# A two-layer hybrid trunk on one core: token differences in other buffers, and two weight splits of each head pair on GpSimd

## What is computed

```
h = rms_norm(x, g);  z = h @ w_in[l]                       # 2048 -> 6400 columns
z_rwkv = z[:, :3328] + (previous token's z - z) * mu       # "token shift"
y_r = rwkv7(r, k, v, decay, a, gate)                       # 16 heads x 64, chunked delta rule
y_a = causal attention with rotary q, k                    # 8 heads x 128, 256 keys
x = x + rms_norm([y_r, y_a] @ w_out[l], g)
x = x + rms_norm(relu(h2 @ w_up[l])**2 @ w_down[l], g)     # 2048 -> 8192 -> 2048
```

## Time and profile before

| | |
|---|---|
| median of 3 runs | 2717.87 us (2716.47 to 2718.49) |
| the profiled execution | 2718.53 us, span 2716.9 us |
| busy share of the span | PE 96%, PEld 79%, DVE 62%, ACT 45%, POOL 4% |
| mean granted TensorE clock | 0.985 |
| DMA | 419.96 MB, 155 GB/s over the span |

### The profile page before, as it was taken

One profiled execution on the slowest core, in us unless ns is written; L12 is line 12 of the kernel. 1 busy time (PEld: TensorE's weight loads), 2 busy tenths in 40 slices (PEclk: granted clock), 3 DMA queues, 4 the chain that ended last, 5 costly groups with the idle time before them and its releaser, 6 DMA issues.

```text
span 2716.9 us, 48417 instructions
## 1 busy us (share of the span) xinstructions
PE 2612.0 (96%) x16267; PEld 2137.8 (79%) x16267; DVE 1680.0 (62%) x2761; ACT 1213.9 (45%) x1896; POOL 116.8 (4%) x183
## 2 busy tenths in 40 slices
PE   7999999999999999999899999999999999999998
PEld 6777777777888888888787777776778888888886
DVE  5666666656656556566566666666576565565665
ACT  5444444445434444444454444444454344344443
POOL 3000000000000000000010000000000000000000
PEclk9999999999999999999999999999999999999999
DMA  6333333355555555555533333333555555555554
GB/s 196 100 110 103 102 102 103 103 179 170 190 195 179 197 191 185 193 186 186 181 112 105 108 97 101 103 103 101 179 164 197 192 186 189 192 185 193 178 196 151
DMA packets 437897, 419.96 MB, mean 155 GB/s; under 512 B 19502, under 2 KB 351936, under 8 KB 437824
## 3 DMA queue, kind: packets, MB, share of 16 engines
q1 hardware_dynamic: 434176, 412.49, 47.8%
q0 software_dynamic: 3648, 6.52, 0.8%
HBM read 416.84 MB, written 2.10 MB: 154 GB/s over the span
## 4 chain that ended last, share of the span: by engine, by line
PE 87%; DVE 7%; issue 2%; ACT 2%; POOL 1%; DVEq 0%; DMA 0%; SPq 0%; ACTq 0%; POOLq 0%
PE gemm_bank L515 27%; PE gemm_bank L516 14%; PE gemm_bank L540 11%; PE gemm_bank L542 11%; PE gemm_bank L541 11%; PE gemm_bank L518 2%; DVE b_wlo L1157 1%; PE mix_banks L662 1%; PE mix_banks L688 1%; ACT b_whi L893 1%; DVE b_rn L1268 1%; PE mix_banks L695 1%; PE mix_banks L734 1%; PE mix_banks L738 1%; PE mix_banks L745 1%
## 5 line engine op out<-in xcount | busy, mean ns | idle before, releaser
L1157 DVE TENSOR_TENSOR b_wlo<-b_raw,b_whi 128x1024 fp32r<-128x1024 f32 x777 | 940.1, 1223 | 593.5 <-ACT b_whi L893 591.3
L515 PE MATMUL gemm_bank<-b_hT,b_whi 128*128 128x512 f32 x3420 | 1268.5, 411 | 5.2 <-DVE b_zt L1163 5.0
L893 ACT ACTIVATE b_whi<-b_raw 128x1024 fp32r<-128x1024 f32 x777 | 810.0, 1057 | 609.9 <-PE gemm_bank L542 423.6
L516 PE MATMUL gemm_bank<-b_hT,b_wlo 128*128 128x256 f32 x3648 | 1018.4, 283 | 0.0
L515 PEld LDWEIGHTS gemm_bank<-b_hT,b_whi 128*128 128x128 f32 x3420 | 649.4, 190 | 177.4 <-issue 24.6
L516 PEld LDWEIGHTS gemm_bank<-b_hT,b_wlo 128*128 128x128 f32 x3648 | 695.8, 191 | 11.5
L540 PE MATMUL gemm_bank<-b_whi,b_mT 128*128 128x512 f32 x1280 | 501.6, 392 | 0.0
L542 PE MATMUL gemm_bank<-b_whi,b_mT 128*128 128x512 f32 x1280 | 498.3, 389 | 0.0
L541 PE MATMUL gemm_bank<-b_wlo,b_mT 128*128 128x512 f32 x1280 | 498.2, 389 | 0.0
L540 PEld LDWEIGHTS gemm_bank<-b_whi,b_mT 128*128 128x128 f32 x1280 | 240.3, 188 | 51.3 <-issue 1.4
L542 PEld LDWEIGHTS gemm_bank<-b_whi,b_mT 128*128 128x128 f32 x1280 | 240.3, 188 | 50.1
(11 more groups left out here) (236 smaller groups left out, 1915.5 us busy)
## 6 DMA issues: line engine op xcount, KB each, us to landing
b_raw<-in_w_up SPq DMA_DIRECT2D x256, 512.0 KB
b_raw<-in_w_down SPq DMA_DIRECT2D x256, 512.0 KB
b_raw<-in_w_in SPq DMA_DIRECT2D x384, 256.0 KB
b_raw<-in_w_out SPq DMA_DIRECT2D x60, 512.0 KB
b_raw<-in_w_in SPq DMA_DIRECT2D x8, 512.0 KB
b_xt<-in_x SPq DMA_DIRECT2D x4, 512.0 KB, 6.0
b_raw<-in_w_out SPq DMA_DIRECT2D x8, 256.0 KB
out<-b_xt SPq DMA_DIRECT2D x8, 256.0 KB, 2.3
```

The lines of the kernel that those rows point to most:

```text
L515: mm(bank[b0 + b][:, :], whi[r][:, cols], pair, start=first, stop=False)
L516: m = mm(bank[b0 + b][:, 0:SEQ], wlo[r][:, cols], act[:, kt, 0, :], start=False, stop=False)
L893: f(whi[r][:, :], raw[r][:, :, :].rearrange("p a b -> p (a b)"), ACT.Copy).then_inc(hi_done, 1)
L1157: tt(wlo[r][:, :], flat(raw[r][:, :, :]), whi[r][:, :].bitcast(F32), ALU.subtract).then_inc(lo_done, 1)
```

## The change

`dsh` becomes three separate buffers: `ta` and `kf` for the two differences of line 441, and the second half of `xs` for the third. The first two are last read at lines 1298 to 1310 of the same pair. `pt` moves to the first 384 columns of `yo`. GpSimd no longer waits for TensorE's transpose (`x_free`) ahead of line 441; the semaphore keeps only its use at the start, under the name `col_zero`. TensorE's `key_norms` moves from behind lines 776 and 777 to ahead of the wait for the probabilities. DVE's `step(-1)` and `step(10)` are gone; GpSimd makes these two `lo` splits of each pair, between the first two differences and the third, each after the matching `hi` and in the order of `lo_done`. DVE waits for both at `step(0)`.

```
-        pt = yof[:, 768:1152]
+        pt = yof[:, 0:384]
-        dsh = yof[:, 0:3 * SEQ].rearrange("p (a b) -> p a b", b=SEQ)
+        dsh = (ta[:, :], kf[:, :], xs[:, 1, :])
...
-            def unit(l, i, n, tiles, after):
+            def unit(l, i, n, tiles, slot, after):
                 pool.wait_ge(tile_out, tiles - 2)
-                pool.wait_ge(e["x_free"], n + 1)
                 for j in (1, 0):
-                    nc.gpsimd.tensor_tensor(dsh[:, j, :], zt[:, j, 0:SEQ], zt[:, j, 1:SEQ + 1],
+                    nc.gpsimd.tensor_tensor(dsh[j], zt[:, j, 0:SEQ], zt[:, j, 1:SEQ + 1],
                                             ALU.subtract).then_inc(e["diffed"], 1)
+                for j in range(2):
+                    pool.wait_ge(hi_done, slot + j + 1)
+                    pool.wait_ge(lo_done, slot + j)
+                    at = (start[l, "pairs"][0] + 9 + j) % ROUND
+                    nc.gpsimd.tensor_tensor(wlo[at][:, :], raw[at][:, :, :].rearrange("p a b -> p (a b)"),
+                                            whi[at][:, :].bitcast(F32), ALU.subtract).then_inc(lo_done, 1)
                 pool.wait_ge(e["pair_done"], n + 1)
                 pool.wait_ge(tile_out, tiles)
...                                        (TensorE, tail of a pair)
                 for u in range(2):
                     m = turned(mb[1][:, P * u:P * u + P], zt[:, 5, 1 + P * u:1 + P * u + P], ident)
-                    m.then_inc(e["va_turned"] if u else e["x_free"], 1)
+                m.then_inc(e["va_turned"], 1)
+                if more:
+                    key_norms(n + 1)
                 pe.wait_ge(e["probs"], V)
...
                 mm(mb[1][:, P:2 * P], vt[:, 1, :], pt[:, 2 * P:3 * P], ...).then_inc(e["o_sum"], 1)
-                if more:
-                    key_norms(n + 1)
                 fill(2)
...                                        (DVE)
                 nc.vector.tensor_tensor_scan(flat(cs[:, :, :]), hp, flat(ldc[:, :, :]), 0.0, ...)
-                step(-1)
...
                 step(9)
-                step(10)
...
                     def step(j):
+                        if j == 0:
+                            dve.wait_ge(lo_done, k + 8 + LEAD + i * 12)
                         lo(k + 8 + j + LEAD, i * 3)
```

More of the change, by code:

```diff
@@ L227, in trunk @@
                  "u_sum", "u_out", "s_sum", "s_tmp", "s_out", "y_sum", "y_mean", "y_cen", "y_sq", "y_var", "y_root",
-                 "y_rinv", "y_norm", "y_turned", "y_gain", "y_bonus", "y_scaled", "y_gated", "y_hi", "x_free",
+                 "y_rinv", "y_norm", "y_turned", "y_gain", "y_bonus", "y_scaled", "y_gated", "y_hi", "col_zero",
                  "swapped", "roped_c", "roped_s", "roped", "va_turned", "va_out", "score_sum", "masked", "smax",
@@ L409, in _ @@
             nc.gpsimd.memset(yof, 0.0).then_inc(clears, 1)
-            nc.gpsimd.memset(ldc[:, :, 0:1], 0.0).then_inc(e["x_free"], 1)
+            nc.gpsimd.memset(ldc[:, :, 0:1], 0.0).then_inc(e["col_zero"], 1)
             nc.gpsimd.memset(St[:, 0, :], 0.0).then_inc(e["pair_done"], 1)
@@ L434, in _ @@
             pair_weights(0, 0)
-            def unit(l, i, n, tiles, after):
+            def unit(l, i, n, tiles, slot, after):
                 pool.wait_ge(tile_out, tiles - 2)
-                pool.wait_ge(e["x_free"], n + 1)
                 for j in (1, 0):
-                    nc.gpsimd.tensor_tensor(dsh[:, j, :], zt[:, j, 0:SEQ], zt[:, j, 1:SEQ + 1],
+                    nc.gpsimd.tensor_tensor(dsh[j], zt[:, j, 0:SEQ], zt[:, j, 1:SEQ + 1],
                                             ALU.subtract).then_inc(e["diffed"], 1)
+                for j in range(2):
[4 more added lines that the diff above has]
+                                            whi[at][:, :].bitcast(F32), ALU.subtract).then_inc(lo_done, 1)
                 pool.wait_ge(e["pair_done"], n + 1)
                 pool.wait_ge(tile_out, tiles)
-                nc.gpsimd.tensor_tensor(dsh[:, 2, :], zt[:, 2, 0:SEQ], zt[:, 2, 1:SEQ + 1],
+                nc.gpsimd.tensor_tensor(dsh[2], zt[:, 2, 0:SEQ], zt[:, 2, 1:SEQ + 1],
                                         ALU.subtract).then_inc(e["diffed"], 1)
@@ L484, in _ @@
                 k, t = start[l, "pairs"]
-                loop(pool, PAIRS - 1, lambda i: unit(l, i, PAIRS * l + i, t + 4 + i * 6,
+                loop(pool, PAIRS - 1, lambda i: unit(l, i, PAIRS * l + i, t + 4 + i * 6, k + 9 + i * 12,
                                                      lambda: pair_weights(l, i + 1)))
-                unit(l, PAIRS - 1, PAIRS * l + PAIRS - 1, t + 6 * PAIRS - 2,
+                unit(l, PAIRS - 1, PAIRS * l + PAIRS - 1, t + 6 * PAIRS - 2, k + 93,
                      lambda: pair_weights(l + 1, 0) if l < DEPTH - 1 else None)
@@ L1250, in key_norms @@
                     dve.wait_ge(e["diffed"], 3 * n + m + 1)
-                    stt(sh[:, j, :], dsh[:, j, :], col(MU + PAIRS * j), zt[:, j, 1:], ALU.mult,
+                    stt(sh[:, j, :], dsh[j], col(MU + PAIRS * j), zt[:, j, 1:], ALU.mult,
                         ALU.add).then_inc(e["shifted"], 1)
@@ L1286, in mixer @@
                 dve.wait_ge(e["diffed"], 3 * n + 3)
-                stt(sh[:, 2, :], dsh[:, 2, :], col(MU + PAIRS * 2), zt[:, 2, 1:], ALU.mult,
+                stt(sh[:, 2, :], dsh[2], col(MU + PAIRS * 2), zt[:, 2, 1:], ALU.mult,
                     ALU.add).then_inc(e["shifted"], 1)
@@ L1473, in parameters @@
                 dve.wait_ge(clears, 2)
-                dve.wait_ge(e["x_free"], 1)
+                dve.wait_ge(e["col_zero"], 1)
             for l in range(DEPTH):
@@ L1504, in _ @@
                 sums(t, 0, place(0))
-                for j in range(3):
+                for j in range(2):
                     lo(k + 4 + LEAD + j)
@@ L1523, in step @@
                 def step(j):
+                    if j == 0:
+                        dve.wait_ge(lo_done, k + 92 + LEAD)
                     if j < 10:
```

## The result

The changed kernel takes 2649.33 us (median of 4 runs, 2648.75 to 2650.53); the kernel before took 2717.49 us beside it (4 runs, 2716.47 to 2718.49). The ratio is 0.975, interval 0.9733 to 0.9767. The profiled execution took 2648.75 us against 2718.53: 69.8 us less, where 69 were forecast; between the medians it is 68.2 us.

A forecast was written before the change was run, and what follows sets the result against it. TensorE, busy 96% of the span, was taken as the bound, leaving only its idle time and half-clock stretches. 41.5 + 22 + 8.5 - 3 = 69 us off 2718.53 gave 2649.5, stated as 2650; range 2637 to 2664.

The forecast's parts named there:

- The stall: TensorE's wait at the transposes of the probabilities, 14 times 3.0 us, goes entirely: 41.5 us.
- Rival C: The stall only moves: key norms' products or line 786 hold TensorE for 2 of 3 us; 2688, chance 0.08.
- What is late next: Tail, line 786, normalised output: a looped pair has about 0.5 us of cover, so no wait, narrowly.
- The clock: Half-clock windows of TensorE behind the stalls vanish with them: 22 us, bounds 0 and 22.
- Rival B: The stall goes but TensorE's clock still falls at the same places for another reason: 2671, chance 0.08.
- Size of GpSimd's split: A 128 x 1024 `lo` split on GpSimd takes 2.45 us, four times the 613 ns row, and stays hidden.
- rival A: Slow splits at the pair's start: 3.9 us each on GpSimd, TensorE waits at line 650; 2686, chance 0.13 with E.
- D: Slower than before: GpSimd's splits above 5.2 us become the chain through the third difference; 2765 at 6 us, chance 0.05.
- E: GpSimd is held by another wait (`lo_done` or `pair_done`) and behaves as rival A; chance 0.13 together with it.
- DVE relieved: Without `step(10)` and `step(-1)`, TensorE's waits shrink: 2.5 us at line 515, 5 at 650, 1 at 640; 8.5 together.
- New contention: In the tail, GpSimd's first differences delay DVE's chunk-state updates by 0.2 us each: 3 us lost, bounds 0 and 8.
- The key norms' move: TensorE's two key-norm products go ahead of the probabilities; costed at nothing in the sum.

The follow-up runs named there:

- busy_stall: Kernel before, plus four throwaway TensorE products of 384 columns in the stall ahead of the probabilities' transposes; 2695.81 us, ratio 0.9919.
- moved_no_gpsimd: Changed kernel with the two splits of a pair back on DVE, key norms' move and new buffers kept; 2647.09 us, ratio 0.9737.
- splits_only: Kernel before with only the two splits of a pair on GpSimd; buffers, transpose wait and key norms' order as before; 2723.19 us, ratio 1.0022.
- floor_early_both: Changed kernel, both splits on GpSimd, with DVE's floor under the key norms moved ahead of `step(9)`; 2652.22 us, ratio 0.9765.
- floor_early_none: Changed kernel with all splits back on DVE and DVE's floor under the key norms moved ahead of `step(9)`; 2641.66 us, ratio 0.9722.

## Why the prediction was right, and where it was wrong

The sum was 41.5 + 22 + 8.5 - 3 = 69, and 69.8 came (68.2 by the medians). By the medians of the runs it is 42.1 (stall) + 22.6 (clock) + 6.7 (key norms moved) - 3.7 (GpSimd's splits), 67.7. It was right in its total because the two large terms were right; that is the mechanism. That the rest came out within 2.5 us (8.5 - 3 = 5.5 forecast, 6.7 - 3.7 = 3.0 measured) is luck: neither of the two terms was what it was taken for.

*The stall.* Right, with both margins near the forecast: GpSimd was 1.1 us ahead of DVE (104.93 and 106.03; 1.1 forecast), and DVE waited 0.98 us for ACT (0.7 forecast). Two signs were misstated, and decide nothing. Line 1251 was to start "some 3.9 us after `zt`"; by the prediction's own times that is 2.3 us after (3.9 or so is how much earlier it comes), and 2.36 was measured. And 64.4 us is the first looped pair's length; the mean was 63.66. Rival C (the stall only moves) is excluded by the missing waits at lines 621 and 778.

*What is late next.* Right: no looped pair waits at line 791, as forecast for line 786.

*The clock.* Right, and shown by busy_stall: 22.6 us against 22. Rival B (no clock) falls.

*Size of GpSimd's split.* Right: 2.38 us against 2.45 from the row of 613 ns. Rivals A and D needed 3.9 us and over 5.2. The third difference was hidden, as the forecast had it: DVE's line 1291 has no wait for it. With that E falls too.

*DVE relieved, 8.5 us.* Wrong. The step that failed is "Removing `step(-1)` brings line 1310 forward by up to 1.2 us". It brought it forward by 1.2 and put it back by 1.4. At line 650, where 5 us were to be won, nothing was (7.1 and 7.1; all eight of these waits are in layer 1); at line 640, where 1 us was, 2.7 were lost. Only the 2.5 us at line 515 came, and even these are not due to `step(10)` alone: moved_no_gpsimd, in which DVE has all its splits, has the same 2.2 us there, from the moved key norms; in splits_only it was the missing `step(10)`.

*New contention, 3 us.* Wrong in its place. It was looked for in the tail, where the chunk-state update at line 1402 takes 0.35 us as it did before: it starts only as GpSimd's second difference ends, and the update ahead of it (line 1399) has an input in PSUM. It lay at the start of the pair, beside the long splits. The prediction had the two rows (613 and 977 ns) and read them as GpSimd's price only; it never asked what the same meeting costs DVE, and called DVE's work there "mostly one-input" and so exempt. The trace of the kernel before already held the answer, in layer 1, where GpSimd's value residual runs beside DVE:

```profile
1417.91 0.48 DVE L1295 SCALAR_TENSOR_TENSOR b_rn<-b_sh,b_drv,b_rn 128x256 f32<-128x256 f32 x1
...
1417.97 1.00 POOL L451 TENSOR_TENSOR b_xs<-b_vf,b_sh 128x256 f32<-128x256 f32 x1 [5.38 <-DVE b_sh L1287]
...
1418.42 0.84 DVE L1298 TENSOR_TENSOR b_ta<-b_rn,b_ta 128x256 f32<-128x256 f32 x1
...
1419.12 0.74 POOL L455 TENSOR_TENSOR b_xs<-b_xs 128x256 f32<-128x256 f32 x1
...
1419.18 0.83 DVE L1305 TENSOR_TENSOR b_AR<-b_rn,b_eP 128x128 f32<-128x128 f32 x1
```

In layer 0, without the residual, lines 1298 and 1305 take 0.50 and 0.28 us. Here the first ends 0.29 us and the second 0.15 us behind a GpSimd instruction that had begun before it. And line 451, begun 0.06 us into DVE's line 1295, ends 0.58 us behind it, about the 0.61 us of the row without such a meeting: the 977 ns hold a wait for one DVE instruction and are not a rate, so rival A's 3.9 us, four times the row, was a wrong reading.

The Trainium skill (SBUF — State Buffer, Who interferes with whom) states it outright: GpSimd and VectorE share a port pair under an exclusive lock, held for a whole instruction, and `tensor_scalar` in its two-port mode takes it as well as an instruction with two SBUF inputs. The rows agree: 0.28 us became 1.87, 0.42 became 2.64, and the reciprocal and the sum with a PSUM input kept their time; no trace here names an instruction's mode. The section of the Trainium skill that the prediction cites (GPSIMD Engine Reference, Specifications) names contention with DVE instructions in a two-port mode as well; the prediction took up only the kind with two SBUF inputs.

*The key norms' move.* A term left at nothing without a price; it brought 6.7 us. The prediction asked only whether it would hold TensorE up, and not who waits for its result: ACT's root, at the head of ACT's queue, ahead of the splits that the next pair starts with.

## What to carry to other kernels

Before giving work to GpSimd, lay its instruction beside DVE's timeline and ask of each DVE instruction under it whether it takes two SBUF inputs or is a `tensor_scalar`: in these runs such a one, begun after GpSimd's, ended only with it, whatever it took alone. Look for a place in the trace at hand where the two engines already meet, and compare DVE's durations there with the same lines elsewhere. Put the GpSimd instruction under a DVE instruction that is long and not of this kind (here a reciprocal), and compare the duration of DVE's groups before and after, since this loss is in no list of waits. When a product is moved, ask of the engine that reads it what is queued behind that read.

## What the runs showed that had not been expected

- The lock in numbers: DVE instructions of 0.23 to 0.42 us lasted up to 2.64 us, until 0.14 to 0.29 us after the end of a GpSimd `tensor_tensor` of 2.4 to 2.5 us. The scan (0.70 us, two SBUF inputs) took 0.96 in the mean beside a GpSimd difference of 0.67 us.
- The same split on GpSimd costs 16.4 us, costs 6.7 us, or brings 7.0 us, by what stands beside it on DVE.
- TensorE idle for 3.0 us was followed by a stretch at 1.2 GHz in 12 of 14 pairs (11 of 14 in splits_only), 22.6 us in all; with throwaway products in the gap, which left 0.4 us of idling, in none.
- floor_early_both loses 10.6 us against floor_early_none where the group means give 0.46 x 16 = 7. The means hide part of it, since they take in shorter cases (line 1279's shortest is 0.52 us). In the looped pair above, line 1279 has 1.82 us for 0.26 and the scan 0.99 for 0.70, and the split that DVE is rid of took 1.12 us from its start to the next instruction's: 0.73 us lost. The periods are 0.70 and 0.65 us longer, 9.5 us over the 14 pairs.
- splits_only loses 4.8 us where the group means give 7 (16 x 0.61, less 2.8 at `zt`). The clock makes up the difference: in windows of 7 us behind its 14 stalls, as in the earlier trace rows, the missing clock adds up to 20.8 us, where it was 23.3 before; by the prediction's 2.72/2.87 that is an estimated 2.4 us of time given back.
- What stays open: why some pairs keep their clock behind a stall of 3.0 us, and by what path the earlier floor of the key norms brings the half of its 4 us that TensorE's waits do not show.
